# Attention in a split-precision transformer kernel: transposed probabilities in two alternating halves, scores of both heads issued together, VectorE's scaling moved ahead of the low halves

## The reference

```python
# first: 8 heads, each with two score maps of depth 64, keys 0..511
s = einsum('bqhd,bkhd->bhqk', qb, k) * scale
pr = softmax(s).reshape(B, H, 2, DIFF_Q_BLOCK, S)
a = pr[:, :, 0] - lam_full * pr[:, :, 1]
o = einsum('bhqk,bkhe->bqhe', a, v)          # e = 128
# second: 16 query heads on 4 key heads, depth 64, |i-j| <= 128, one sink logit a head
m = maximum(max(s), sink); e = exp(s - m)
pr = e / (sum(e) + exp(sink - m))
# third: 8 heads, depth 64, causal, with forgetting
s = einsum("bhqd,bhkd->bhqk", qi, kh) * scale + ci[..., :, None] - c[:, :, None, :]
p = softmax(where(k_pos <= q_pos, s, -inf))
```

## Time and profile before

| | us |
|---|---|
| runs, median of 3 (lowest, highest) | 2368.62 (2357.4, 2379.38) |
| the profiled execution, first to last instruction (its span) | 2358.1 |
| TensorE busy in it (share) | 2166.2 (92%) |
| VectorE busy | 1364.2 (58%) |
| ScalarE busy | 984.0 (42%) |
| GpSimd busy | 813.8 (35%) |

### The profile page before, as it was taken

How to read it: one execution, slowest core, us unless ns; L and a number is a source line. 1 busy time by engine, 2 the same in 40 slices (tenths; PEclk the granted TensorE clock), 3 DMA queues, 4 the chain that set the end, 5 groups by cost and what they waited for, 6 DMA issues and landing times. The chain is left out here.

```text
span 2358.1 us, 27415 instructions
## 1 busy us (share of the span) xinstructions
PE 2166.2 (92%) x9442; PEld 1730.2 (73%) x9442; DVE 1364.2 (58%) x1850; ACT 984.0 (42%) x1549; POOL 813.8 (35%) x332
## 2 busy tenths in 40 slices
PE   6899889999999889989999999887979799999999
PEld 5666558788887667768878887665667578888887
DVE  5477756726274757656736456647868946423323
ACT  4566534524244455444524334433642143422222
POOL 3321114444444320004544445342102434444443
PEclk9999789999999988979999999989989899999999
DMA  3111002222222210002222223121101122222223
GB/s 143 72 36 45 27 21 105 98 99 98 98 95 93 72 54 28 19 10 99 98 98 96 101 90 116 63 81 63 36 18 54 63 79 92 98 98 94 94 97 107
DMA packets 49920, 179.61 MB, mean 76 GB/s; under 512 B 5536, under 2 KB 5664, under 8 KB 49824
## 3 DMA queue, kind: packets, MB, share of 16 engines
q1 hardware_dynamic: 48384, 174.09, 21.0%
q10 hardware_dynamic: 1440, 4.21, 0.5%
HBM read 176.18 MB, written 2.10 MB: 76 GB/s over the span
## 5 line engine op out<-in xcount | busy, mean ns | idle before, releaser
L459 POOL TENSOR_TENSOR wlo<-raw,whi 128x1024 fp32r<-128x1024 f32 x328 | 813.5, 2484 | 1529.4 <-ACT whi L902 1529.2
L466 PE MATMUL PS<-Bhi,whi 128*128 128x512 f32 x2368 | 946.8, 400 | 65.3 <-DVE Blo L1381 19.8
L466 PE MATMUL PS<-Blo,whi 128*128 128x512 f32 x2368 | 934.3, 395 | 0.0
L466 PE MATMUL PS<-Bhi,wlo 128*128 128x512 f32 x2368 | 933.2, 394 | 0.0
L466 PEld LDWEIGHTS PS<-Bhi,whi 128*128 128x128 f32 x2368 | 453.1, 191 | 182.9 <-issue 39.6
L902 ACT ACTIVATE whi<-raw 128x1024 fp32r<-128x1024 f32 x328 | 345.3, 1056 | 536.2 <-PE PS L466 458.3
L466 PEld LDWEIGHTS PS<-Bhi,wlo 128*128 128x128 f32 x2368 | 452.1, 191 | 96.5
L466 PEld LDWEIGHTS PS<-Blo,whi 128*128 128x128 f32 x2368 | 453.1, 191 | 93.7 <-issue 2.2
L1372 DVE TENSOR_TENSOR AR<-PS,R 128x512 f32<-128x512 f32 x172 | 116.6, 689 | 204.1 <-PE PS L466 188.2
L1422 DVE TENSOR_TENSOR X<-X,PS 128x512 f32<-128x512 f32 x96 | 66.0, 688 | 228.9 <-PE PS L466 227.7
L1620 DVE SCALAR_TENSOR_TENSOR AR<-AR,par_sb 128x511 f32<-128x511 f32 x88 | 150.4, 1709 | 13.4 <-DVE AR L1617 3.9
(11 more groups left out here) (195 smaller groups left out, 2254.5 us busy)
## 6 DMA issues: line engine op xcount, KB each, us to landing
raw<-in_weights SPq DMA_DIRECT2D x328, 512.0 KB, 3.2
X<-in_xT ACTq DMA_DIRECT2D x4, 512.0 KB, 8.2
out<-X SPq DMA_DIRECT2D x8, 256.0 KB, 2.6
AR<-in_pT ACTq DMA_DIRECT2D x2, 512.0 KB, 3.2
con_sb<-in_constants ACTq DMA_DIRECT2D x1, 333.0 KB, 9.2
par_sb<-in_parameters ACTq DMA_DIRECT2D x1, 322.0 KB, 5.0
AR<-in_positions ACTq DMA_DIRECT2D x1, 256.0 KB, 9.4
AR<-in_lambdas ACTq DMA_DIRECT2D x1, 128.0 KB, 9.2
```

Of the source, the lines that this page charges most:

```text
L459: pool.tensor_tensor(wlo[:, j, :], raw[:, j % RAWS, :], f32(whi[:, j, :]), ALU.subtract).then_inc(lo_ready, 1)
L466: return pe.matmul(out, w, x, start=start, stop=stop)
```

## The change

`pthi` and `ptlo` grow from 4 to 6 rows of 512 and are used as two halves, one for even and one for odd groups (`keys_of`, `row_of`); GROUP is 2 in all three attentions, so a head of the first has two products of 256 columns instead of one of 512; `prob_high` waits for the product two groups back. In kinds 2 and 3 the scores' matmuls of both maps are issued in a row and the masks behind them. On VectorE `normalise(g+1)` stands ahead of `prob_low(g)`. `minusR` becomes one column a head, repeated by its access pattern.

```diff
--- before.py
+++ after.py
@@ -196,8 +196,8 @@
         Blo = [sb(f"Blo{n}", [P, KC * T], F32R) for n in range(2)]
         qkhi = sb("qkhi", [P, 2, 2, T], F32R)
         qklo = sb("qklo", [P, 2, 2, T], F32R)
-        pthi = sb("pthi", [P, 4, T], F32R)
-        ptlo = sb("ptlo", [P, 4, T], F32R)
+        pthi = sb("pthi", [P, 6, T], F32R)
+        ptlo = sb("ptlo", [P, 6, T], F32R)
         R = sb("R", [P, T])
         acc = sb("acc", [P, T])
         sq = sb("sq", [P, 2, T])
@@ -207,7 +207,7 @@
         par_sb = sb("par_sb", [P, NPAR])
         con_sb = sb("con_sb", [P, NCON])
         constR = sb("constR", [P, 3, P], F32R)
-        minusR = sb("minusR", [P, 8, P], F32R)
+        minusR = sb("minusR", [P, 8], F32R)
         cc = sb("cc", [P, T], F32R)
         wfhi = sb("wfhi", [P, KC * 8], F32R)
         wflo = sb("wflo", [P, KC * 8], F32R)
@@ -358,8 +358,8 @@
 
         SC0 = {1: 0, 2: 64, 3: 128}
         PB0 = {1: 0, 2: 32, 3: 96}
-        GROUP = {1: 4, 2: 2, 3: 2}
-        PV0 = {1: 0, 2: 8, 3: 24}
+        GROUP = 2
+        PV0 = {1: 0, 2: 16, 3: 32}
         OP0 = {1: 0, 2: 8, 3: 16}
         QT0 = {1: 0, 2: 16, 3: 26}
 
@@ -413,16 +413,26 @@
                 return QT0[2] + 2 + t, t % 2 if t else 1, 0 if t else 1
             return QT0[3] + t, (t // 2) % 2, t % 2
 
+        def keys_of(buf, kind, g):
+
+            v, half = buf.rearrange("p a t -> p (a t)"), g // GROUP % 2
+            lo, n = {1: (1024 * half, 4), 2: (1536 * half, 6), 3: (2048 * (1 - half), 4 + 4 * half)}[kind]
+            return v[:, lo:lo + n * 2 * P].rearrange("p (r c) -> p r c", c=2 * P)
+
+        def row_of(kind, g, s, k):
+
+            if kind == 1:
+                return k
+            qb = g % 4
+            base = band(kind, qb - qb % 2)[0]
+            return (3 if kind == 2 else 2 + 2 * (g // GROUP % 2)) * s + k - base
+
         def transposed(buf, kind, g, s):
 
 
-            qb = g % 4
-            first, nb, _ = band(kind, qb)
-            if kind == 1:
-                return buf[:, :, qb * P:qb * P + P]
-            k0 = 4 * s + first - band(kind, qb - qb % 2)[0]
-            c = qb % 2 * P
-            return buf.rearrange("p a (b c) -> p (a b) c", c=2 * P)[:, k0:k0 + nb, c:c + P]
+            first, nb, _ = band(kind, g % 4)
+            r, c = row_of(kind, g, s, first), g % 2 * P
+            return keys_of(buf, kind, g)[:, r:r + nb, c:c + P]
 
         def head_of(j, s):
 
@@ -627,6 +637,7 @@
                     if kind == 3 and j == 0:
 
                         pe.wait_ge(cc_ready, 1)
+                outs = []
                 for s in range(2):
                     n = SC0[kind] + 2 * g + s
                     back = {1: 2, 2: 4, 3: 3}[kind]
@@ -642,9 +653,15 @@
                     out = PS[:, score_bank(kind, n), 0:nb * P]
                     last = mm3(out, qkhi[rows, b, 0, cols], qklo[rows, b, 0, cols],
                                qkhi[rows, kb, 1, keys], qklo[rows, kb, 1, keys], True, kind == 1)
+                    if kind == 1:
+                        last.then_inc(score_done, 1)
+                    outs.append(out)
+                if kind == 1:
+                    return
+                for s, out in enumerate(outs):
                     if kind == 3:
-
-                        mm(out, minusR[:, 2 * j + s, :], cc[:, keys], False, False)
+                        h = 2 * j + s
+                        mm(out, minusR[:, h:h + 1].broadcast_to((P, P)), cc[:, keys], False, False)
                     for q, (at, mask) in enumerate(masks):
                         last = mm(out[:, at * P:at * P + P], identR, mask, False, q == len(masks) - 1)
                     last.then_inc(score_done, 1)
@@ -671,35 +688,29 @@
                 heads = HP[kind]
 
                 pe.wait_ge(pt_ready, PB0[kind] + heads * (g + 1))
-                if last_qb == GROUP[kind] - 1 and OP0[kind] + j:
+                if last_qb == GROUP - 1 and OP0[kind] + j:
 
                     pe.wait_ge(o_ready, OP0[kind] + j)
                 nh = {1: 8, 2: 4, 3: 8}[kind]
                 vhi = Bhi[1][:, 0:TB * nh * P].rearrange("p (k n c) -> p k n c", k=TB, n=nh)
                 vlo = Blo[1][:, 0:TB * nh * P].rearrange("p (k n c) -> p k n c", k=TB, n=nh)
-                if kind == 1:
-                    work = [(k, 0, TB, 0) for k in range(TB)]
-                else:
-
-
-                    q0 = last_qb - 1
-                    spans = []
-                    for k in range(TB):
-                        qs = [q for q in (q0, last_qb)
-                              if band(kind, q)[0] <= k < band(kind, q)[0] + band(kind, q)[1]]
-                        if qs:
-                            spans.append((len(qs) == 2, k, qs[0], qs[-1] + 1))
-                    spans.sort(reverse=True)
-                    work = [(k, a, b, 0) for _, k, a, b in spans]
+                q0 = last_qb - 1
+                spans = []
+                for k in range(TB):
+                    qs = [q for q in (q0, last_qb)
+                          if band(kind, q)[0] <= k < band(kind, q)[0] + band(kind, q)[1]]
+                    if qs:
+                        spans.append((len(qs) == 2, k, qs[0], qs[-1] + 1))
+                spans.sort(reverse=True)
+                work = [(k, a, b, 0) for _, k, a, b in spans]
+                if kind != 1:
+
+
                     work += [(k, a, b, 1) for _, k, a, b in reversed(spans)]
                 for n, (k, a, b, s) in enumerate(work):
                     head = {1: j, 2: 2 * (j // 4) + s, 3: 2 * j + s}[kind]
-                    if kind == 1:
-                        xs = [buf[:, k, :] for buf in (pthi, ptlo)]
-                    else:
-                        row = 4 * s + k - band(kind, q0)[0]
-                        xs = [buf[:, row // 2, (row % 2) * 2 * P + (a - q0) * P:
-                                  (row % 2) * 2 * P + (b - q0) * P] for buf in (pthi, ptlo)]
+                    r, c = row_of(kind, g, s, k), (a - q0) * P
+                    xs = [keys_of(buf, kind, g)[:, r, c:c + (b - a) * P] for buf in (pthi, ptlo)]
                     last = mm3(PS[:, 7, a * P:b * P], vhi[:, k, head, :], vlo[:, k, head, :],
                                xs[0], xs[1], n == 0, n == len(work) - 1)
                 last.then_inc(pv_done, 1)
@@ -747,7 +758,7 @@
                         for h in SPREAD.get(g, ()):
                             spread_factor(h)
                     transposes(kind, g)
-                    if g and g % GROUP[kind] == 0:
+                    if g and g % GROUP == 0:
                         outputs(kind, g - 1)
                     if kind == 3 and finished(kind, g - 1) is not None:
                         head_sums(finished(kind, g - 1))
@@ -1030,15 +1041,16 @@
                     n = PB0[kind] + HP[kind] * g + s
 
                     act.wait_ge(trans_done, n + 1)
-                    if PV0[kind] + g // GROUP[kind]:
-                        act.wait_ge(pv_done, PV0[kind] + g // GROUP[kind])
+                    if g // GROUP >= 2:
+
+                        act.wait_ge(pv_done, PV0[kind] + g // GROUP - 1)
                     act.activation(transposed(pthi, kind, g, s), PS[:, 2 + n % 2, 0:blocks * P]
                                    .rearrange("p (k q) -> p k q", k=blocks), ACT.Copy)\
                        .then_inc(pthi_ready, 1)
 
             def evacuate(kind, j):
 
-                act.wait_ge(pv_done, PV0[kind] + (j + 1) * (4 // GROUP[kind]))
+                act.wait_ge(pv_done, PV0[kind] + (j + 1) * (4 // GROUP))
                 act.activation((OA3 if kind == 3 else OA)[:, j, :], PS[:, 7, :], ACT.Copy)\
                    .then_inc(o_ready, 1)
 
@@ -1571,9 +1583,9 @@
                 steps = 4 * PAIRS[kind]
                 for g in range(AHEAD[kind]):
                     maxima(kind, g)
+                normalise(kind, 0)
                 for g in range(steps):
                     begun, halfway = finished(kind, g - 1), finished(kind, g - 2)
-                    normalise(kind, g)
                     if g + AHEAD[kind] < steps:
                         maxima(kind, g + AHEAD[kind])
                     if kind < 3 and begun is not None:
@@ -1592,6 +1604,8 @@
                             norm_output(h)
                         for h in SPREAD.get(g - 1, ()):
                             normed_low(h)
+                    if g + 1 < steps:
+                        normalise(kind, g + 1)
                     prob_low(kind, g)
                     if kind == 2:
                         for c in OSPLIT.get(g, ()):
@@ -1685,8 +1699,7 @@
             dve.wait_ge(con_in, 16)
             dve.tensor_copy(constR[:, :, :], con_sb[:, 0:3 * P].rearrange("p (n c) -> p n c", n=3))\
                .then_inc(consts_ready, 1)
-            dve.tensor_copy(minusR[:, :, :], con_sb[:, CCOLS["minus"][0]:CCOLS["minus"][1]]
-                            .rearrange("p (n c) -> p n c", c=1).broadcast_to((P, 8, P)))\
```

(2 more changed lines are left out.)

## The result

The changed kernel takes 2279.82 us in the median of four runs (2274.89 to 2283.01) against 2369.11 for the kernel before: ratio 0.9607, interval 0.9566 to 0.9647. Timed again beside two groups of experiments it had 2276.84 (0.9615) and 2278.77 (0.9617). With 2370 us for the kernel before that is 91 to 93 us. I had forecast 69 and 2300 us, inside a range of 2272 to 2342: direction and range held, the gain is a third larger. By the profiled executions it is 79.8, since the one of before was a quick one (a span of 2358.1 us).

What follows compares the result with a forecast made beforehand. The prediction took the three attentions to be bound by the order in which engines wait for each other. Gains of 30, 28 and 11 us sum to 69, from 2368.6 to 2300 us, inside a range of 2272 to 2342.

Steps and rivals of the forecast that it cites:

- The walk: First attention: counting one head's engine work in order, ending with ScalarE late, gave 22.0 us; 23.0 was forecast.
- The last steps: End of the first attention, steps without projection: waits for products go and the last product halves, gaining 6 us.
- Second attention: Four steps go from 23.5 to 19.8 us, gaining 22; the eight last steps gain 6; together 28 us.
- Third attention: Bound by VectorE: four collisions go for 8 us, later steps lose waits for products for 3; together 11 us.
- A collision costs 2.0 us: VectorE's scaling meeting GpSimd's subtraction over SBUF loses about 2.0 us in each of seventeen long rows, 34 in all.
- Part 1's doubling of the products: First attention: 24 short product matmuls a head instead of 12 cost 3.02 instead of 2.94 us, 0.7 in the whole kernel.
- Part 2's cover: VectorE: the moved scaling is mostly over before GpSimd's subtraction; the low half and maxima behind it read PSUM.
- Part 3: Scores in a row save TensorE 16 us in the second attention, 8 in the third; alone worth half or less.
- The collisions stay: Rival, chance 0.12: the 2.0 us beside GpSimd's subtraction is only paid elsewhere on VectorE; gain 35, 2334 us.
- ScalarE becomes the bound: Rival, chance 0.13: ScalarE's copies and roundings hold the exponentials, only the 27 waits are won; gain 28, 2341 us.
- The low half becomes the last: Rival, chance 0.03: VectorE is held in normalise(g+1) while the ready low half stands behind; 22 us slower, 2391 us.
- Everything closes up: Rival, chance 0.08: TensorE's sums bound all three attentions and the clock stays at 2.4 GHz; gain about 100, 2268 us.

Runs made afterwards that it cites:

- e11: Changed kernel with the first attention's output copy, square, sum, root and reciprocal one step later, timed again in six runs: 2271.01 us, ratio 0.9586.
- e2: Changed kernel with the masks again behind each map's own scores in the second and third attention: 2292.02 us, ratio 0.9654.
- e4: Kernel before with only VectorE's order changed, normalise(g+1) ahead of prob_low(g): 2313.82 us, ratio 0.9733.
- e5: Kernel before with GpSimd subtracting only 64 of 1024 columns in the 28 slabs rounded during the attentions: 2322.47 us, ratio 0.9814.
- e6: Changed kernel with GpSimd subtracting only 64 of 1024 columns in the 28 slabs rounded during the attentions: 2276.02 us, ratio 0.9608.
- e10: Changed kernel with the scaling back behind the low half and masks behind each map's scores, leaving only the two halves: 2344.49 us, ratio 0.9877.
- e8: Changed kernel with the first attention's output copy, square, sum, root and reciprocal one step later, first timing: 2274.33 us, ratio 0.9597.

## Why the prediction was right, and where it was too small

**What bounded the kernel** was right. The order of the waits bound the three attentions, and all of the gain is there: 33.3, 35.6 and 17.0 us by the low halves, where I had 30, 28 and 11. The rest of the span is 6.1 us longer in that profile and 2.4 in the repetition's. Other borders don't explain it: from the first exponential to the last product matmul the gains are 34.5, 35.6 and 16.2 us, and the rest is 6.5 longer. 2.6 us of it lie between the second and third attention, in both profiles. What takes them is open.

**First attention, a head.** The walk gave 22.0 us, and the head took that. I added a microsecond "for hand-overs that it leaves out" and took 23.0. That was the mis-sized term: 6 x 1.0 = 6 us. The last steps gave about 3 instead of 6. ScalarE was rightly the late engine: VectorE waits 2.43 us for the copies at 199.21, and e11 wins 0.9 a head by relieving it. The walk had TensorE wait 0.9 us for the exponentials; measured, it loses 0.9 there, as scores that no longer pair. That the whole is exact has some luck in it: 11.8 + 4.2 is 16.0 and not 15.8, the products take 0.2 more than assumed, and of a second delay by ScalarE in the head, with which the walk ended, the rows show none in TensorE, whose later scores pair again at 206.40 and 210.69.

**Second attention.** I took 19.8 for four steps, and they took 19.3 (in the repetitions too): 3 us of the missing 7.6. (TensorE's terms add up to 19.5 and not 19.6, which changes nothing.) The other part is at its beginning and end, where I had 6: 35.6 - 6 x 4.2 = 10. The kernel before had stood at half clock for long there (a mean of 0.84 in the earlier trace rows against 0.91 in the regular part, shown above).

**Third attention.** 17.0 instead of 11. Taking the scores in a row away costs 8.0 of it (e2), and the order alone wins 8.5 (e4). I had given the collisions 8 and the waits for products 3, and the scores no term of their own in this stage.

**A collision costs 2.0 us** was the wrong size, in the row rather than in the sum. "Each loses about 2.0 us, 34 in all": the instruction does, but e5 gives 44 us in all. In three heads of the kernel before the price was the gap and then matmuls at 1.2 GHz, 3.0 us; where the clock held it was 1.5. I had put half a microsecond of slow clock into four steps and nothing into a head.

**Part 1's doubling of the products** cost more than 0.7 us: 12 matmuls of 256 columns take 192.84 to 194.44, 1.60 us, so a head has 3.20 instead of 2.94, 2 us in the whole kernel. The starts are 0.12 apart, and 0.20 at either end of the row; the 0.126 of the forecast was a mean over matmuls of 256 and of 128 columns. The sign of over 0.15 did not show. The 32 weight loads from one repeated column cost nothing, as forecast: 186 ns in the median before and 185 in e2, which has the same order. The Trainium skill ("TensorE: Matmul & The Clock Gate", Back-to-back issue gap), by whose figures I had estimated 7 us, is not borne out by these rows either.

**Part 2's cover** was right in the first attention: the scaling is over before GpSimd starts, and behind it stand readers of PSUM. In the second it missed the minimum with the sinks, a reader of SBUF behind the maxima, which now takes 1.65 us in six rows. The Trainium skill ("GPSIMD Engine Reference", 1. Specifications) says that the two contend for SBUF; e5 and e6 agree, since shortening GpSimd's instruction alone takes the long rows away in the kernel before (all but one), and those of the minimum in the kernel after, where it wins nothing.

**Part 3** was undersold. "By itself it would be worth half or less": done alone it is worth 17 us of the 24 of TensorE's work that the forecast gave it, all in the second attention, and 9 to 11 on top of the others.

**The sum.** Alone the parts win 63, 17 and 29 us, 109 together; in one kernel they win 91 to 93. Taken away last, the order costs 27 to 29 us, the halves' looser wait 11 to 14 and the scores 9 to 11: the parts overlap, probably since each fills gaps that the others fill too. That the base was the median and the span was 10.5 below it did no harm: the gain by medians is larger than the one by the profiled spans.

**The rivals.** "The collisions stay" was a quarter true in the rows, six of them by 1.5 us each, and wrong in the time: e6 takes these away and four steps go from 19.3 to 19.2. "ScalarE becomes the bound" was half true: it is what holds the head at 22.0, for 6 to 8 us in all, and not for the 41 that this rival took off the gain. "The low half becomes the last" showed outside the regular parts: TensorE's transposes wait 14.1 us for low halves, which was one of my signs of being wrong, but of the 46.5 that their matmuls had waited for the scaling 5.5 are left. "Everything closes up", 2268 us, was nearer than I gave it credit for: in the middle of the first attention TensorE is busy all the time at full clock. The signs I named: the wait under 20 us, no scaling row over 1 us, score matmuls in pairs and four steps in about 20 came true; "heads of 22.5 to 23.5" did not, and neither did "clocks of 0.92 or more in the three windows" (0.91, 0.89, 0.87). In the regular parts they are 1.00 and 0.97, and the slow clock is now at the ends of the stages.

## What to carry to other kernels

If a chain walked through row by row ends at 22.0, forecast 22.0: a margin for what might be left out is a guess, and here it was wrong by its whole size. Price a stall of TensorE as the stall and, where the clock falls, the slow matmuls behind it, and judge a row of waits by what else runs meanwhile: 29 us more of waiting were worth 11 to 14. When an instruction is moved away from a collision, look at what then stands in its place. Try parts alone as well as together, since their sum can be larger than the whole and one of them can look like a loss in one stage.

## What the runs showed of the hardware that I had not expected

A VectorE instruction of 0.75 us with two inputs in SBUF that meets a GpSimd subtraction of 2.6 us takes 2.76 us, and even one on 128x2 values takes 1.65 instead of 0.16. With an input in PSUM it keeps its time: 30 of the 172 rows of L1384 fall on a subtraction and take 0.69 us as the others do. A head of the first attention with such a collision is 1.5 us longer where the clock holds and 3.0 where it falls. The change touches the attentions alone: in the gated MLPs of the kernel after 44 of the 88 rows of L1634 take 2.65 us instead of 0.75 beside GpSimd, and what that is worth was not tried.

The same matmuls of the second attention (about 890 in the records) in the same order keep TensorE busy for 160 us (e2), 175 (before) or 193 (e10) at mean clocks of 0.91, 0.84 and 0.76. And two executions of one kernel (e8 and e11) differ by 7 us in one place, where TensorE waited 4.25 us in one of them and its clock fell behind it, 0.74 against 1.00.
